# A hybrid attention and recurrence layer: another order of TensorE's work where the two recurrences end

## The reference

```python
def hgrn2_chunkwise(q, f, i):
    b = jnp.cumsum(logf, axis=2)
    q_dec = q * jnp.exp(b)
    k_inv = k * jnp.exp(-b)
    a = jnp.where(causal, jnp.einsum('bnthk,bnshk->bnhts', q_dec, k_inv), 0.0)
    o_intra = jnp.einsum('bnhts,bnshv->bnthv', a, v)
    u = jnp.einsum('bnshk,bnshv->bnhkv', k_out, v)
    def step(state, xs):
        d, u_c = xs
        return d[..., None] * state + u_c, state
    _, s_before = lax.scan(step, s0, ...)
    o_inter = jnp.einsum('bnthk,bnhkv->bnthv', q_dec, s_before)
    return (o_intra + o_inter).reshape(B, S, H, dv)

def hybrid_layer(...):
    h = rms_norm(x, norm_w) * (1.0 + scale[:, None]) + shift[:, None]
    proj = h @ w_in
    ...
    rec = rms_norm(rec, rec_norm_w).reshape(B, S, REC_WIDTH) * jax.nn.silu(rg)
    mixed = jnp.concatenate([attn, rec], axis=-1) @ w_out
    return x + gate[:, None] * mixed
```

## Time and profile before

| | |
|---|---|
| median of three executions | 1812.95 us (1811.62 to 1813.28) |
| the profiled execution's own time | 1813.45 us |
| its span, first to last instruction | 1811.7 us |
| PE busy | 1775.8 us, 98% of the span |
| DVE busy | 1293.6 us, 71% |
| ACT busy | 973.6 us, 54% |
| POOL busy | 481.5 us, 27% |
| mean granted clock of PE | 0.996 of full speed |

### The profile page before, as it was taken

One profiled execution on the slowest core, in us unless ns is written; L12 is line 12 of the kernel. 1 busy time (PEld: TensorE's weight loads), 2 busy tenths in 40 slices (PEclk: granted clock), 3 DMA queues, 4 the chain that ended last, 5 costly groups with the idle time before them and its releaser, 6 DMA issues.

```text
span 1811.7 us, 28428 instructions
## 1 busy us (share of the span) xinstructions
PE 1775.8 (98%) x9856; PEld 1507.4 (83%) x9856; DVE 1293.6 (71%) x2692; ACT 973.6 (54%) x2127; POOL 481.5 (27%) x825
## 2 busy tenths in 40 slices
PE   6999999999999999999999999999999999999999
PEld 4788888888878888878888888887888888888887
DVE  7966476777767666696646777776786657987987
ACT  5622225777776565552222577877556555343441
POOL 1000026667722222200002567773222220000000
PEclk9999999999999999999999999999999999999999
DMA  9142322221223444344133222121432248278252
GB/s 359 70 163 96 114 105 100 74 71 40 86 68 118 123 136 133 106 168 163 75 123 109 105 75 65 46 86 33 156 127 80 72 145 313 83 250 295 107 180 93
DMA packets 158494, 222.30 MB, mean 123 GB/s; under 512 B 11792, under 2 KB 104336, under 8 KB 150672
## 3 DMA queue, kind: packets, MB, share of 16 engines
q1 hardware_dynamic: 158352, 220.49, 36.0%
HBM read 163.18 MB, written 57.28 MB: 122 GB/s over the span
## 4 chain that ended last, share of the span: by engine, by line
PE 88%; DVE 5%; DMA 2%; issue 2%; POOL 1%; ACT 1%; SPq 0%; DVEq 0%; POOLq 0%; ACTq 0%
PE bank L902 68%; PE bank L1059 3%; PE bank L1048 3%; PE bank L1080 3%; PE bank L1110 2%; PE bank L1128 2%; PE bank L1143 1%; PE bank L1106 1%; PE bank L1012 1%; PE bank L1156 1%; PE bank L1133 1%; DMA o_lower<-mixed_cols 1%; DVE g_lo L1795 1%; DMA ob_raw<-in_w_out 0%; PE bank L1097 0%
## 5 line engine op out<-in xcount | busy, mean ns | idle before, releaser
L902 PE MATMUL bank<-h_hi,w_hi 128*128 128x512 f32 x512 | 205.9, 402 | 0.2
L902 PE MATMUL bank<-h_lo,w_hi 128*128 128x512 f32 x512 | 199.9, 390 | 0.0
L902 PE MATMUL bank<-h_hi,w_lo 128*128 128x512 f32 x512 | 199.6, 390 | 0.0
L902 PE MATMUL bank<-wq_hi,h_hi 128*128 128x384 f32 x512 | 176.9, 346 | 0.5 <-issue 0.5
L902 PE MATMUL bank<-ob_hi,oa_hi 128*128 128x512 f32 x448 | 175.0, 391 | 1.0 <-DVE ua L2232 0.8
L902 PE MATMUL bank<-ob_hi,oa_lo 128*128 128x512 f32 x448 | 174.4, 389 | 0.0
L902 PE MATMUL bank<-ob_lo,oa_hi 128*128 128x512 f32 x448 | 174.3, 389 | 0.0
L902 PE MATMUL bank<-wq_hi,h_lo 128*128 128x384 f32 x512 | 171.9, 336 | 0.0
L902 PE MATMUL bank<-wq_lo,h_hi 128*128 128x384 f32 x512 | 171.1, 334 | 0.0
L1324 ACT ACTIVATE g_hi<-g_raw 128x2048 fp32r<-128x2048 f32 x36 | 69.0, 1916 | 162.4 <-PE bank L902 156.4
L1480 ACT ACTIVATE sm<-sm,neg_m 128x257 f32<-128x257 f32 x256 | 127.4, 504 | 18.0 <-DVE neg_m L2046 18.0
(11 more groups left out here) (256 smaller groups left out, 4695.8 us busy)
## 6 DMA issues: line engine op xcount, KB each, us to landing
g_raw<-in_w_in SPq DMA_DIRECT2D x24, 1024.0 KB, 6.2
raw<-in_w_in SPq DMA_DIRECT2D x16, 1024.0 KB, 8.1
o_lower<-mixed_cols SPq DMA_DIRECT2D x32, 512.0 KB, 6.7
nat_rows<-u SPq DMA_DIRECT2D x48, 256.0 KB, 2.6
raw<-in_w_in SPq DMA_DIRECT2D x8, 1536.0 KB, 6.5
o_upper<-in_w_out SPq DMA_DIRECT2D x24, 512.0 KB, 9.0
wa<-in_w_ada SPq DMA_DIRECT2D x8, 1024.0 KB, 10.7
g_q<-gate_cols SPq DMA_DIRECT2D x64, 128.0 KB, 2.4
```

The lines of the kernel that those rows point to most:

```text
L902: mm = pe.matmul(dst, a, b, start=(first and m == 0), stop=(last and m == 2), **more)
```

## The change

Two pieces of PE's order change, and nothing else: no instruction is added or removed, and the lists of DVE, ACT, POOL and SP are the same.

- In step 16 of the first recurrence, `gemm_p1(1, 0, 1)` and `chunk_products` of quad 15 now come in front of `outputs` of quad 14. Before, the order was `outputs`, `chunk_products`, `gemm_p1(1, 0, 1)`.
- In `last_quads`, `out_part(0, 0, 1, 0)` now comes in front of `outputs` of quad 14, and no longer behind it. `chunk_products` stood in front of it already.

```diff
@@ last_quads
                 out_part(0, 0, 0, 0)
                 out_part(0, 0, 0, 1)
                 chunk_products(SEGS - 1, T - 1, t - 1)
+                out_part(0, 0, 1, 0)
                 outputs(T - 2, t - 2)
-                out_part(0, 0, 1, 0)
                 chunk_states(SEGS - 1, T - 1, t - 1)
@@ recurrence
                         mix_transposes(s, t - 3)
+                    if t == REC_T:
+                        gemm_p1(s + 1, 0, 1)
+                        chunk_products(s, T - 1, t - 1)
                     if t >= 2:
                         outputs(T - 2, t - 2)
-                    if 2 <= t <= REC_T:
+                    if 2 <= t < REC_T:
                         chunk_products(s, T - 1, t - 1)
@@
-                    if t == REC_T and s + 1 < SEGS:
-                        gemm_p1(s + 1, 0, 1)
                     if 1 <= t <= REC_T:
                         chunk_states(s, T - 1, t - 1)
```

## The result

The changed kernel takes 1816.16 us in the median of 14 executions (1812.69 to 1817.50); the kernel before, beside it, 1812.32 us (14 executions, 1811.14 to 1816.94). The ratio is 1.0018, 95% interval [1.0009, 1.0026], so 3.3 us more, between 1.6 and 4.7. By the prediction's bound of 0.2% that is no change, but it isn't zero. The forecast was 1814.8 us, with 1811.7 to 1817.6 as the range.

The account below looks back on a forecast made before the run. The prediction took the kernel to be bound by PE's matmuls except where PE waits. Its terms, -1.27 + 3.06 = +1.8 us, on 1812.95 us gave 1814.8 us, with a range of 1811.7 to 1817.6.

Parts of the forecast that it names:

- the prediction's bound of 0.2%: Whole kernel: the least change a measurement can tell, about 0.2% or 3.6 us; anything smaller counts as no change.
- First place: First recurrence's end: PE's 2.53 us idle goes, DVE's path brings g_lo and the GEMM's second product 1.27 us earlier.
- DVE's holes: First recurrence's end: DVE's waits of 1.03 us before the masking and 0.27 before carry_states of quad 15 both close.
- Kept to the end: After the first recurrence's end: the 1.27 us gain is kept, since from 795.28 PE runs 212.20 us without a wait.
- Second place, step by step: Second recurrence's end: out_part waits 2.14 us for ob_lo, o_ok comes 3.59 later, DVE's masking 3.06 us later.
- After that nothing gives it back: From the second recurrence's end on, PE and the chain through SP's load both move by the same 3.06 us.
- The rival, the low clock at the second place: Second recurrence's end: clock falls after PE's 2.14 us idle, 1.7 us more, +3.5 in all; chance 0.17.
- A second fall: Second recurrence's end: clock falls also after the 1.6 us state wait, another 0.9 us; +4.4 in all, 1817.4 us.
- The sum: Whole kernel: -1.27 + 3.06 = +1.8 us, forecast 1814.8 us, judged no change.
- the likeliest case: Whole kernel: the forecast without a clock fall at the second recurrence's end, 1813.8 to 1815.6 us; chance 0.64.

Follow-up runs that it names:

- version with a ready part: Kernel before with out_part(0, 0, 0, 2), operands long ready, pulled in front of outputs of quad 14 in last_quads; 1815.00 us, ratio 1.0004.
- second place alone: Kernel before with only out_part(0, 0, 1, 0) moved in front of outputs of quad 14; 1818.97 us, ratio 1.0032; once more 1816.27 us, 1.0021.
- first place alone: Kernel before with only gemm_p1(1, 0, 1) and chunk_products of quad 15 moved in front of outputs of quad 14; 1812.82 us, ratio 0.9996.
- `k_nat` early: As first place alone, but in step 16 ACT's copy k_nat stands in front of the squares of quad 14; 1812.52 us, ratio 0.9997.
- chunk products alone: Kernel before with only chunk_products of quad 15 moved in front of outputs of quad 14, gemm_p1(1, 0, 1) staying behind; 1812.96 us, ratio 0.9997.

## Why the prediction was right, and where it was off

- **First place, -1.27: the size and the path are right, the reason is half right.** The stage gave 1.56 less in the two first profiles, and 1.56 less over all (18.09 in the mean of six with the new order, 19.65 of eight with the old). From `weights_t1` to `g_lo` DVE takes 784.92 - 773.75 = 11.17 us against 12.49: 1.32, where 1.27 were forecast. The second product then follows `g_lo`'s start by 2.38 us and no longer 2.79, for 0.41 more, which I hadn't counted; 0.17 are lost ahead of `weights_t1`. The two waits came as told: 1.72 for `k_nat` (forecast 1.9) and 0.54 for `g_lo`; 1.2 were forecast for that one, but PE arrived 0.5 us later behind the transposes than forecast and the product came 0.3 earlier. But the prediction took DVE's holes for a result of the order, and they follow from the clock. The rows before say so: at full speed the chunk products would have ended at 773.38 + 0.90 + 1.06 = 775.34, ahead of `weights_t1`'s end at 776.14. One profile shows it: where the clock stayed up in the old order (2.04 us wait), the hole was not there and the stretch took 17.65, as short as with the move. So the move is worth the fall of the clock that it prevents, which came in seven of the eight profiles with the old order.
- **Kept to the end: right for this pair, not in each execution.** Between the two first profiles the long stretch up to the attention is equal to 0.02 us. The prediction read that PE doesn't wait from 795.28 on the earlier trace rows, and passed over the stretch from 789.13 to there. In that stretch PE can come to wait for `r_mix`, and in two of the six profiles with the move this took about 1.1 of the 1.56 us. 1.3 are kept in the mean. That this meets the forecast's 1.27 is luck: the stage gave more than was forecast, and the next one takes some of it back.
- **Second place, step by step: right.** Counted from the start of the transposes L1133, the part starts 2.58 us later after the change and 2.57 before. The masking comes 3.19 later than before (forecast 3.06), with 3.09 us idle. `o_rinv` took 1.87 us again, so `mix_rows` and the state moved by the same 3.19; the wait for the state was 1.40 (forecast 1.6). The version with a ready part confirms what was argued from `ob_lo`: 2.2 of it is that wait.
- **"After that nothing gives it back": right in the mean, not in the pair.** Between these two profiles, 3.19 became 2.52 at the end: the old wait for `ua` shrank from 0.78 to 0.19 us, and the chain's load took 9.59 us in place of 10.25. But that wait is 0 to 0.87 us in the old order by the execution, and against the mean of eight (315.20) the three profiles with the move and the clock up (318.15) lose 2.95. The forecast's 3.06 stands.
- **The rival, the low clock at the second place: its mechanism exists, its price was right, how often it comes is open.** +1.7 was forecast. 16.80 - 15.20 = 1.60 was measured up to L1110 of quad 15, and 319.88 - 318.15 = 1.73 to the end. It came in one of four profiles with the move, and in none of the two of the whole change. A second fall, behind the 1.40 us, came in none.
- **The sum.** By the profiles it is -1.3 + 2.95 = +1.6 with the clock up, +3.4 with it down; +1.8 was forecast, and +3.3 [1.6, 4.7] measured. So the forecast lies near the lower end of the interval, and what makes the rest, if it is one, stays open. The low clock at the second place, which the likeliest case left out, suggests itself, but the mean granted clock of the executions speaks against it. A fall like that of the earlier trace rows, 3.5 us at 0.51, lowers it by 0.001. The second place alone has 0.9956 in the mean of 15 executions, against 0.9964 of 80 of the kernel before: nearly one fall more in each. But the whole change has 0.9968 (25), as much as three versions without the second place's move have (first place alone, `k_nat` early, chunk products alone), 0.9969 (33). Beside each other on one chip, the whole change took 1816.58 us and the last two of these 1812.52 and 1812.96, with the same mean clock of 0.9968: 3.6 to 4.1 us for the second place, where the profiles with the clock up have 2.95. Single executions say little on it: the kernel before took 1818.59 us in the execution that was profiled once more, with 3.6 us more up to the transposes of quad 13 and 1.4 more in the recurrence's middle, places that no version touches.

The Trainium skill (TensorE: Matmul & The Clock Gate, "Why this matters for your kernels") warns of a fallen clock only for idle gaps longer than the 2.00 us behind which it fell to 0.50 here. The trace doesn't agree with it, as at the first place, and the measurement decides.

The Trainium skill (GPSIMD Engine Reference, "1. Specifications") says that GpSimd's interfaces to SBUF are shared with VectorE, with contention when DVE reads two inputs from SBUF. The trace agrees: `o_rinv` took 1.87 us beside `ob_lo`, which reads two, and 1.01 us at 1514.70, while DVE stood idle.

## What to carry to other kernels

Before a group of matmuls goes in front of others, ask for each of its operands when it is there. Six matmuls whose operands were ready cost the end nothing that showed, and six behind a late `ob_lo` cost it 3 us, since what they pushed back releases another engine's list. Where a wait like the 2.35 to 2.70 us here stands in front of dense work, look at the granted clock behind it: to prevent its fall can be the whole gain of a move. And compare stages over several profiles before a difference in one of them is given to the change: a load's landing, with the clock that fell behind it, moved a stage by up to 2.6 us here.

## What the runs showed of the hardware that was not expected

- The same load of 1536 KB landed in 6.61 to 8.66 us at the same place of versions that do not differ there. Up to 7.14 us it is hidden; from 7.60 us on it costs 0.4 to 0.9 us, and 2.0 to 2.6 where the clock fell behind PE's wait.
- The length of PE's wait alone doesn't tell whether the clock falls. At the two places of the change, waits of 1.98, 1.98, 2.02 and 2.04 us had no fall behind them and one of 2.00 had; all seven of 2.35 to 2.70 us had one. At the attention's start, waits of 1.67, 2.20, 2.22 and 2.23 us had one, and 1.75 and 2.17 had none.
- After a fall the half clock cost 1.6 to 1.7 us where 3.3 us of matmuls stood behind it, and it spread to DVE, whose next work waited for them: the masking 4.67 us in place of 3.09.
- POOL's `o_var`, 128x4, took 0.19 to 0.46 us when it started ahead of DVE's 2.29 us `s_f`, and 1.95 to 2.35 us when it started with it or up to 0.4 us behind.
